# A triangular solve in 32x32 diagonal blocks in place of 64x64 chunks, and an MLP loop written out

## The chip, the cores and the metric

The kernel runs on one core of a Trainium2 chip. Its time is device microseconds (us) of one execution; the kernel before takes 2452.07 us, the median of three runs (2451.09 to 2452.88). The core has a matrix engine (TensorE, PE in the rows, with its weight loads shown apart as PEld), VectorE (DVE), ScalarE (ACT), GpSimd (POOL) and SyncE (SP), which issues the DMAs.

## What is computed

Two transformer-like layers run over 256 tokens of width 2048, all in float32. The first holds a gated delta rule (8 heads of 128), a Fourier branch, and an MLP of width 8192; the second holds a spatial gate, a state space model and an attention over a memory. The part that the change touches is the delta rule, and there the solve:

```
def gated_delta_rule_chunked(q, k, v, g, beta):      # chunks of 64 tokens
    ...
    m = jnp.where(strict, jnp.einsum("bhnid,bhnjd->bhnij", kb, k) * decay, 0.0)
    a_mat = m + jnp.eye(CHUNK, dtype=m.dtype)
    rhs = jnp.concatenate([v * beta, kb * jnp.exp(gc)[..., None]], axis=-1)
    sol = lax.linalg.triangular_solve(a_mat, rhs, left_side=True, lower=True, unit_diagonal=True)
```

There are 4 chunks of 64 tokens, 8 heads and two directions (the reverse one runs over flipped tokens): 64 triangular matrices of 64x64, each with ones on its diagonal. The kernel inverts each and multiplies by the inverse in the scan. The MLP is `x + square(relu(h @ w_mlp_up)) @ w_mlp_down`.

## The kernel before

All weights stream from HBM once, in 396 units of 512 rows by 512 columns (1 MB). SyncE loads a unit into one of four buffers `raw`; ScalarE rounds it into `w_hi` (line 820), VectorE makes the rest `w_lo` (line 1272), and TensorE multiplies each unit in 24 matmuls of 128x512 (lines 2098 to 2100: high by high, low by high, high by low; two tiles of 128 tokens). All engines walk the same list of units, `n` from 0 to 395. Between the two halves of a unit each engine runs the steps that `schedule()` put at that place; `delta_steps(half)` is the list of the delta rule's steps, and it is run twice, for heads 0 to 3 and 4 to 7 (`half`). So in each engine's queue the solve is a short group of instructions between matmuls of the weight stream.

The inverse X of a unit lower triangular matrix is built by doubling. With the blocks of size s already inverted, X of size 2s is X - X M' X, where M' is what M has in the lower left s x s block of each 2s block. `LEVELS` is (1, 2, 4, 8, 16, 32). Level 0 is done with a mask (`turn`, lines 1584 to 1599 on VectorE: unit minus masked M, for X and for its transpose). Each of the levels n = 1 to 5 has two steps:

- `solve_y` (TensorE line 2291): Y = M'X, for t = 0 and 1. GpSimd has masked M' with `level` beforehand (line 1190), ScalarE copies Y out of PSUM (line 1019).
- `solve_x` (line 2300): two products for each t, XMX transposed and XMX, and VectorE subtracts both (lines 1606 and 1609), since both X and its transpose are needed on the next level. On the last level the transposed one alone is made, and GpSimd scales it into `solT` (line 1195), which the scan reads.

One t holds two chunks, one in partitions 0 to 63 and one in 64 to 127, and 8 columns of blocks (4 heads, 2 directions). `by_chunk` (line 2256) issues for each of the 8 the two chunks' products, 16 matmuls of 64x64 for one t. The chunk in the lower partitions uses one quarter of TensorE's array and the other the quarter diagonally across. A float32 matmul of this kind is recorded as two passes, each a weight load and a matmul: 16 matmuls are x32 in the rows. `turn` on TensorE transposes M and the matrix ATT with `by_chunk` against the identity, before level 1.

Every group begins by waiting for semaphores (`take_bank` for one of the four PSUM banks, then the operands). Once they are met TensorE's queue runs it with nothing between.

The MLP is cut in 8 pieces. Of its units, 96 are run as a loop in hardware (`drive`, `LOOP0`, `LOOPS` = 3 turns of `LOOP_UNITS` = 32 units); waits in it add the turn's number times a constant to their value, and a few waits are left out in it.

Of the kernel before, what the change touches and what calls it, by code (L numbers as in the profile page):

```python
# [40 lines left out]
LEVELS = (1, 2, 4, 8, 16, 32)  # L41
MAGIC = 12582912.0
# [52 lines left out]
def end(name, n):  # L95
# [15 lines left out]
         ("chunk", 256), ("upto", 192), ("unit", 64), ("level", 896),  # L111
# [10 lines left out]
def mask_constants():  # L122
# [10 lines left out]
    out["unit"] = packed(r == c)  # L133
    out["level"] = np.concatenate([packed(x) for m in lower for x in (m.T, m)] +
                                  [packed(lower[0]), packed(lower[0].T)], 1)
# [29 lines left out]
def schedule():  # L165
# [67 lines left out]
    put(end("w_mlp_up", 2 * p), "hidden", p, 0)  # L233
    put(end("w_mlp_up", 2 * p + 1), "hidden", p, 1)
# [48 lines left out]
LOOP0 = FIRST[INDEX[("w_mlp_up", 2)]]  # L283
LOOP_UNITS = 32
LOOPS = 3


class Side:
# [3 lines left out]
    def __init__(self, key, eng, sems, old, new):  # L292
        self.key, self.eng, self.sems, self.old, self.new = key, eng, sems, old, new
        self.count, self.it, self.per = 0, None, None
# [8 lines left out]
    def _in_loop(self, key, value):  # L303
        return value if self.it is None else value + self.it * self.per[key]

# [3 lines left out]
    def at(self, *names):  # L309

        marks = [self.old[n] if self.old else ("act", 1) for n in names]
        assert len({key for key, _ in marks}) == 1, names
        return self._in_loop(marks[0][0], max(value for _, value in marks))

    def here(self):

        assert self.count > 0
        return self._in_loop(self.key, self.count)
# [5 lines left out]
def build(nc, t_in, out, old, new):  # L324

    with ExitStack() as ctx:
# [25 lines left out]
        small = take("small", [P, NSMALL - 896])  # L352
        levels = take("levels", [P, 896], mybir.dt.bfloat16)
# [13 lines left out]
        level = levels[:, :].rearrange("p (n d c) -> p n d c", d=2, c=64)  # L367
# [31 lines left out]
        level_in = at("level_in", bb + 16 * KB, [P, 896])  # L399
# [105 lines left out]
        by_head = lambda mask: mask.unsqueeze(2).broadcast_to([P, 2, 4, 64])  # L505
# [72 lines left out]
        def value(me, static, per):  # L578
            return static if me.it is None else static + me.it * per

        def drive(me, slot_work, after_loop):

            n = 0
            while n < UNITS:
                if n == LOOP0:
                    start = me.count
                    me.per = {k: v for k, v in (old or {}).get("per", {}).items()} if old else \
                        {"act": 0, "dve": 0, "pe": 0, "pool": 0}
                    with me.eng.Fori(0, LOOPS) as it:
                        me.it = it  # L590
                        for m in range(LOOP_UNITS):
                            slot_work(n + m)
                    me.it = None
                    per = me.count - start
                    new.setdefault("per", {})[me.key] = per
                    me.count += per * (LOOPS - 1)
                    for j in range(2):
                        for key, x in (("act", "hi"), ("dve", "lo")):
                            if me.key == key:
                                new[f"hidden{NPIECE - 2}.{j}.{x}"] = (key, me.count)  # L600
                                for k in range(NT):
                                    new[f"hidden{NPIECE - 2}.{j}.{k}.{x}"] = (key, me.count)
                    after_loop()
                    n += LOOPS * LOOP_UNITS
                    continue
                slot_work(n)
                n += 1

        def run_steps(me, steps, place):
            if 2 * LOOP0 <= place < 2 * (LOOP0 + LOOP_UNITS):  # L610
                local = (place - 2 * LOOP0 - 1) / 2
                for s, piece, j in ((4, 1, 0), (8, 1, 1), (20, 2, 0), (24, 2, 1)):
                    if local == s:
                        steps["hidden"](piece, j)
                return
# [12 lines left out]
        def _(sp):  # L628
            me = Side("sp", sp, done, old, new)

            def weight(n, it=None):

                if n >= RAW:
                    value = n - RAW + 1
                    sp.wait_ge(pe_used, value if it is None else value + it * LOOP_UNITS)
                if it is None:
                    src = t_in["w"][n]
                else:
                    src = t_in["w"][bass.ds(n + it * LOOP_UNITS, 1)].rearrange("a p n -> (a p) n")
                sp.dma_start(raw[:, n % RAW, :], src).then_inc(landed[n % RAW], 16)  # L640
# [141 lines left out]
            n = 0  # L782
            while n < UNITS:
                if n == LOOP0:
                    with sp.Fori(0, LOOPS) as it:
                        for m in range(LOOP_UNITS):
                            weight(n + m + RAW, it)
                    n += LOOPS * LOOP_UNITS
                    run_steps(me, steps, 2 * n)
                    run_steps(me, steps, 2 * n + 1)  # L790
                    continue
# [6 lines left out]
                n += 1  # L798
                if n != LOOP0 and n not in ends:
                    run_steps(me, steps, 2 * n)  # L800
                    run_steps(me, steps, 2 * n + 1)
# [8 lines left out]
        def _(act):  # L810
# [4 lines left out]
            def split(n):  # L815

                act.wait_ge(landed[n % RAW], value(me, 16 * (n // RAW + (n % RAW > 0)), 16 * LOOP_UNITS // RAW))
                if n >= HIGH:
                    act.wait_ge(pe_used, value(me, n - HIGH + 1, LOOP_UNITS))
                act.activation(w_hi[:, n % HIGH, :], raw[:, n % RAW, :], ACT.Copy)\  # L820
                   .then_inc(hi_split, 1)
# [7 lines left out]
            def job(tag, j):  # L829
# [9 lines left out]
                if mode == "square":  # L839
                    if ts_user[k] and me.it is None:  # L840
# [37 lines left out]
            def empty(i):  # L878
# [3 lines left out]
                act.wait_ge(pe_used, value(me, FIRST[i + 1], LOOP_UNITS))  # L882
                norm = "x" if i <= INDEX[("w_gate_a", 3)] else "mlp" if name == "w_mlp_up" else \
                    "mem" if name.startswith("xa_w") else "pre"
                if n == 0 and me.it is None:
# [118 lines left out]
            def turn(half):  # L1004
# [4 lines left out]
                for t in range(NT):  # L1009
                    act.wait_ge(pe_done, me.at(f"turn{half}{t}.Q"))  # L1010
# [3 lines left out]
            def solve_y(half, n):  # L1014
                for t in range(NT):
# [3 lines left out]
                    act.activation(per_chunk(t)[MAT], bank_of(f"solveY{half}{t}{n}", 0), ACT.Copy)\  # L1019
# [102 lines left out]
            def after_loop():  # L1122
                ts_user[:] = [f"hidden{NPIECE - 2}.1.0"] * 2

            drive(me, slot_work, after_loop)
# [5 lines left out]
        def _(pool):  # L1131
# [47 lines left out]
            def turn(half):  # L1179
                for t in range(NT):  # L1180
                    pool.wait_ge(act_done, me.at(f"turn{half}{t}.MT"))
                    pool.wait_ge(pe_done, me.at(f"decay{half}{t}.D"))
                    pool.tensor_tensor(pairs(per_chunk(t)[SUM]), pairs(per_chunk(t)[MATT]), by_head(level[:, 1]), ALU.mult)\
                        .then_inc(pool_done, me.done(f"solve{half}{t}1.Mt"))

            def solve_x(half, n):
                for t in range(NT):
                    if n < len(LEVELS) - 1:
                        pool.wait_ge(pe_done, me.at(f"solve{half}{t}{n}.Y"))
                        pool.tensor_tensor(pairs(per_chunk(t)[SUM]), pairs(per_chunk(t)[MATT]), by_head(level[:, n + 1]),  # L1190
                                           ALU.mult).then_inc(pool_done, me.done(f"solve{half}{t}{n + 1}.Mt"))
                    else:
                        pool.wait_ge(dve_done, me.at(f"solve{half}{t}{n}.XT", f"bk1{half}"))
                        for d in range(2):
                            pool.tensor_tensor(solT[:, t, 4 * d:4 * d + 4], pairs(per_chunk(t)[EXP])[:, d],
                                               wide(bk1[:, nt(t, d)], 64), ALU.mult)\
# [60 lines left out]
            for n in range(UNITS):  # L1257
                if not LOOP0 <= n < LOOP0 + LOOP_UNITS:
                    run_steps(me, steps, 2 * n)
                    run_steps(me, steps, 2 * n + 1)  # L1260
# [3 lines left out]
        def _(dve):  # L1264
# [4 lines left out]
            def split(n):  # L1269

                dve.wait_ge(hi_split, value(me, n + 1 - EARLY, LOOP_UNITS))
# [141 lines left out]
            def empty(i):  # L1413
# [3 lines left out]
                dve.wait_ge(pe_used, value(me, FIRST[i + 1], LOOP_UNITS))  # L1417
                if me.it is not None or name[:10] == "w_mlp_down" or name == "w_o":

                    dve.wait_ge(dve_emptied, value(me, emptied(i, "dve") - NT, 8 * NT))  # L1420
# [163 lines left out]
            def turn(half):  # L1584
                dve.wait_ge(dve_done, me.here())
                for t in range(NT):
                    w = per_chunk(t)
                    dve.tensor_tensor(pairs(w[INV]), pairs(w[MAT]), by_head(level[:, 6]), ALU.mult)\
                        .then_inc(dve_done, me.done())
                    dve.wait_ge(act_done, me.at(f"turn{half}{t}.MT"))  # L1590
                    dve.tensor_tensor(pairs(w[EXP]), pairs(w[MATT]), by_head(level[:, 0]), ALU.mult)\
                        .then_inc(dve_done, me.done())
                dve.wait_ge(dve_done, me.here())
                for t in range(NT):
                    w = per_chunk(t)
                    dve.tensor_tensor(eight(w[INV]), many(cols["unit"], 8), eight(w[INV]), ALU.subtract)\
                        .then_inc(dve_done, me.done(f"turn{half}{t}.X"))
# [979 lines left out]
```

## Time and profile before

| | us |
|---|---|
| median of 3 runs | 2452.07 |
| the profiled execution, its time | 2454.28 |
| its span, from first to last instruction | 2452.5 |
| TensorE busy | 2429.2 |
| VectorE, ScalarE, GpSimd busy | 1534.6, 1030.0, 274.8 |

The durations in the section of rows are of the one profiled execution. Its time is 1.8 us over its span and 2.2 us over the median. "Busy" for TensorE counts a matmul from its start to its end, and matmuls overlap in the pipeline, so durations of single matmuls (0.22 to 0.4 us) say nothing of the rate. The rate is read from the chain, where each piece runs from its start to the next one's.

### The profile page before, as it was taken

Reading aid. Unit: us, or ns where it says so; the run is one execution under the profiler, and the core shown is the slowest. Engines: PE = TensorE matmul, PEld = TensorE weight load, DVE = VectorE, ACT = ScalarE, POOL = GpSimd, SP = SyncE. Lnnn points to the kernel's source line nnn. Section 1 sums busy time; section 2 is a strip of 40 time slices with the busy share of each in tenths; the row PEclk is TensorE's granted clock in tenths of the full one; section 3 lists DMA queues with packets and bytes.
Section 4 is the critical chain, followed back from the end, with each engine's and each line's share of the span. In section 5 each row is a group of like instructions: output and inputs, shape, how many; then the busy total and the mean of one; then the engine's idle time right before and its main releaser. Section 6 shows DMA issues by size and latency. Waiting matters only on the chain.

```text
span 2452.5 us, 31953 instructions
## 1 busy us (share of the span) xinstructions
PE 2429.2 (99%) x13482; PEld 1996.0 (81%) x13482; DVE 1534.6 (63%) x1530; ACT 1030.0 (42%) x860; POOL 274.8 (11%) x226
## 2 busy tenths in 40 slices
PE   8999999999999999999999999999999999999998
PEld 7888888878888888888888888887777778888886
DVE  6465556557676455445445567789999955446564
ACT  4553345334344443443443434443433444544332
POOL 1002201210000000000000000054556400000000
PEclk9999999999999999999999999999999999999999
DMA  6343354346755455555555555665555576566753
GB/s 257 135 164 115 136 184 168 108 149 245 262 193 184 177 189 190 188 189 191 186 191 194 187 196 205 224 242 192 189 187 194 187 284 234 173 240 227 257 197 137
DMA packets 84220, 475.10 MB, mean 194 GB/s; under 512 B 8704, under 2 KB 8832, under 8 KB 32512
## 3 DMA queue, kind: packets, MB, share of 16 engines
q1 hardware_dynamic: 84096, 473.32, 54.2%
q8 instruction: 94, 1.54, 0.2%
q14 instruction: 30, 0.25, 0.0%
HBM read 450.21 MB, written 23.07 MB: 193 GB/s over the span
## 4 chain that ended last, share of the span: by engine, by line
PE 96%; DMA 1%; DVE 1%; ACT 1%; issue 0%; SPq 0%; DVEq 0%; ACTq 0%
PE acc L2098 29%; PE acc L2100 29%; PE acc L2099 29%; PE banks L2262 3%; PE banks L2111 2%; PE banks L2318 1%; DMA raw<-in_w 1%; PE banks L2385 1%; PE banks L2398 1%; DVE w_lo L1272 0%; ACT w_hi L820 0%; DMA av<-spilled 0%; DVE stats L1324 0%; PE banks L2438 0%; PE banks L2420 0%; PE banks L2236 0%
## 5 line engine op out<-in xcount | busy, mean ns | idle before, releaser
L1272 DVE TENSOR_TENSOR w_lo<-raw,w_hi 128x2048 fp32r<-128x2048 f32 x394 | 908.1, 2308 | 552.7 <-ACT w_hi L820 551.5
L820 ACT ACTIVATE w_hi<-raw 128x2048 fp32r<-128x2048 f32 x394 | 751.8, 1914 | 591.0 <-DMA raw<-in_w 588.8
L2098 PE MATMUL acc<-w_hi,a_hi 128*128 128x512 f32 x2112 | 840.5, 398 | 5.8 <-DVE a_lo L1308 3.1
L2099 PE MATMUL acc<-w_lo,a_hi 128*128 128x512 f32 x2112 | 824.7, 390 | 0.0
L2100 PE MATMUL acc<-w_hi,a_lo 128*128 128x512 f32 x2112 | 824.4, 390 | 0.0
L2098 PEld LDWEIGHTS acc<-w_hi,a_hi 128*128 128x128 f32 x2112 | 397.3, 188 | 104.2 <-issue 15.3
L2100 PEld LDWEIGHTS acc<-w_hi,a_lo 128*128 128x128 f32 x2112 | 397.4, 188 | 84.9
L2099 PEld LDWEIGHTS acc<-w_lo,a_hi 128*128 128x128 f32 x2112 | 397.8, 188 | 78.5
L2098 PE MATMUL acc<-w_hi,b_hi 128*128 128x512 f32 x928 | 364.2, 392 | 0.0
L2100 PE MATMUL acc<-w_hi,b_lo 128*128 128x512 f32 x928 | 361.5, 390 | 0.0
L2099 PE MATMUL acc<-w_lo,b_hi 128*128 128x512 f32 x928 | 361.2, 389 | 0.0
L2100 PEld LDWEIGHTS acc<-w_hi,b_lo 128*128 128x128 f32 x928 | 174.2, 188 | 36.5
L2099 PEld LDWEIGHTS acc<-w_lo,b_hi 128*128 128x128 f32 x928 | 174.4, 188 | 35.3
L2098 PEld LDWEIGHTS acc<-w_hi,b_hi 128*128 128x128 f32 x928 | 174.3, 188 | 35.1
L1252 POOL MEMSET c_out<- 128x2048 f32 x1 | 1.8, 1810 | 1029.1 <-DMA spilled<-stage_b 1029.1
L907 ACT ACTIVATE stage<-acc,stats 128x512 f32<-128x512 f32 x72 | 45.6, 685 | 128.3 <-PE acc L2100 123.8
L1436 DVE TENSOR_TENSOR x_rows<-x_rows,acc 128x512 f32<-128x512 f32 x72 | 46.2, 683 | 39.0 <-PE acc L2100 39.0
L1222 POOL TENSOR_TENSOR rot<-pow_a,pow_b 128x256 f32<-128x256 f32 x32 | 47.5, 1486 | 175.9 <-DVE s_out L1871 130.6
L1857 DVE TENSOR_TENSOR_SCAN prod<-rad,prod 128x256 f32<-128x256 f32 x64 | 56.9, 948 | 0.6
L2098 PE MATMUL acc<-w_hi,m_hi 128*128 128x512 f32 x128 | 50.6, 395 | 0.0
L2099 PE MATMUL acc<-w_lo,m_hi 128*128 128x512 f32 x128 | 50.5, 395 | 0.0
L2100 PE MATMUL acc<-w_hi,m_lo 128*128 128x512 f32 x128 | 50.5, 394 | 0.0
(356 smaller groups left out, 1642.4 us busy)
## 6 DMA issues: line engine op xcount, KB each, us to landing
raw<-in_w SPq DMA_DIRECT2D x395, 1024.0 KB, 4.8
spilled<-stage SPq DMA_DIRECT2D x72, 256.0 KB, 6.0
gate_in<-spilled SPq DMA_DIRECT2D x20, 512.0 KB, 5.8
x_rows<-in_x SPq DMA_DIRECT2D x4, 512.0 KB, 8.2
x_rows<-in_x SPq DMA_DIRECT2D x1, 2048.0 KB, 9.2
mem_rows<-in_mem SPq DMA_DIRECT2D x2, 1024.0 KB, 5.8
spilled<-stage_b SPq DMA_DIRECT2D x8, 256.0 KB, 5.9
out<-y_rows SPq DMA_DIRECT2D x3, 512.0 KB, 2.7
```

The lines of the kernel that those rows point to most:

```text
L820: act.activation(w_hi[:, n % HIGH, :], raw[:, n % RAW, :], ACT.Copy)\
L907: act.activation(dst, src, func, scale=rms(norm, t)).then_inc(act_emptied, 1)
L1222: pool.tensor_tensor(c_[:, g], pa[0][:, g], pb[0][:, g], ALU.mult).then_inc(pool_done, me.done())
L1272: dve.tensor_tensor(w_lo[:, n % RAW, :], raw[:, n % RAW, :], w_hi[:, n % HIGH, :].bitcast(F32), ALU.subtract).then_inc(lo_split, 1)
L1436: ins = dve.tensor_tensor(x_rows[:, t, cs], x_rows[:, t, cs], src, ALU.add)
L1857: dve.tensor_tensor_scan(pr[z + 1][:, g], r_, pr[z][:, g], 0.0, ALU.mult, ALU.add)\
L2098: pe.matmul(o, hi[:, tk], wh, start=first, stop=False)
L2099: pe.matmul(o, hi[:, tk], wl, start=False, stop=False)
L2100: ins = pe.matmul(o, lo[:, tk], wh, start=False, stop=last)
L2111: ins = pe.transpose(b[:, q * P:(q + 1) * P], src(q), ident)
L2262: ins = pe.matmul(b[rs, cs], lhs[rs, cs], rhs(k, rs), start=True, stop=True)
L2318: ins = pe.matmul(b(d, rs)[:, hd * P:(hd + 1) * P], lhs(d, t, rs, hd), rhs(d, rs, hd), start=True, stop=True)
```

## The change

The matrices are cut in their 32x32 diagonal blocks up to level 4, and TensorE takes each block as a matmul of its own. A 128-partition tile holds four strips of 32 partitions, so four blocks lie on the array's diagonal. Levels 1 to 4 need no more than the diagonal blocks, and `by_block` makes 32 matmuls of 32x32 where `by_chunk` made 16 of 64x64. The last level has one block product for each matrix and goes by `across`, which reads one strip and writes its neighbour: 16 matmuls of 32x32. `turn` now makes the transposed blocks, copies of the blocks, and (`turnC`) the lower left blocks transposed.

VectorE has X and its transpose side by side in one tile of 512 columns, and subtracts both in one instruction for each t (two before). ScalarE copies 256 columns of Y instead of 512, GpSimd masks 256 instead of 512. GpSimd clears `solT` on level 1 and scales the diagonal blocks into it in 8 instructions on 32 partitions after level 4; VectorE scales the last level's blocks into it in 8 more. The mask constants shrink from 896 to 384 columns. `drive` now writes all units out, with all waits.

```diff
-        level = levels[:, :].rearrange("p (n d c) -> p n d c", d=2, c=64)
+        level0 = levels[:, 0:128].rearrange("p (x c) -> p x c", c=32)
+        level = lambda n: levels[:, 64 + 64 * n:128 + 64 * n].rearrange("p (d c) -> p d c", c=32)
+        strip = lambda g: slice(32 * g, 32 * g + 32)
...
-        def drive(me, slot_work, after_loop):
...
-                    with me.eng.Fori(0, LOOPS) as it:
...
+        def drive(slot_work):
+            for n in range(UNITS):
                 slot_work(n)
...
+            def by_block(b, at, lhs, rhs):
+                for k in range(8):
+                    for g in range(4):
+                        ins = pe.matmul(b[strip(g), at + 32 * k:at + 32 * k + 32], lhs(k, strip(g)), rhs(k, strip(g)),
+                                        start=True, stop=True)
+                return ins
+            def across(b, at, lhs, rhs, to):
+                for hd in range(4):
+                    for c in range(2):
+                        for d in range(2):
+                            first, second = strip(2 * c + d), strip(2 * c + 1 - d)
+                            src, dst = (first, second) if to == "second" else (second, first)
+                            ins = pe.matmul(b[dst, at + 32 * hd:at + 32 * hd + 32], lhs(d, hd, src), rhs(d, hd, src),
+                                            start=True, stop=True)
+                return ins
...
             def solve_y(half, n):
...
-                    by_chunk(b, w[SUM], lambda k, rs: w[INV][rs, 64 * k:64 * k + 64], f"solve{half}{t}{n}.Y")
+                    if n < LAST:
+                        ins = by_block(b, 0, lambda k, rs: block_of(w[SUM], k, rs), lambda k, rs: x_n(w, k, rs))
+                    else:
+                        ins = across(b, 0, lambda d, hd, rs: block_of(w[MAT], hd, rs), lambda d, hd, rs: x_n(w, 4 * d + hd, rs),
+                                     "second")
...
             def solve_x(half, n):
...
+                    if n < LAST:
+                        by_block(b, 0, y, lambda k, rs: x_t(w, k, rs))
+                        ins = by_block(b, 256, lambda k, rs: x_t(w, k, rs), y)
+                    else:
+                        ins = across(b, 0, lambda d, hd, rs: y(8 + hd, rs), lambda d, hd, rs: x_t(w, 4 * d + hd, rs), "first")
```

TensorE's queue at the first `turn`, before; `banks` is PSUM, `work_b` and `work_c` hold the matrices, `small` the identity:

```order
734 L2262 MATMUL banks<-small,work_b 64x64 x16
735 L2262 MATMUL banks<-small,work_c 64x64 x16
736 L2262 MATMUL banks<-small,work_b 64x64 x16
737 L2262 MATMUL banks<-small,work_c 64x64 x16
738 L2098 MATMUL acc<-w_hi,a_hi 128x512
```

and the same place of the changed kernel:

```order
734 L2245 MATMUL banks<-small,work_b 32x32 x32
735 L2245 MATMUL banks<-work_b,small 32x32 x32
736 L2245 MATMUL banks<-small,work_c 32x32 x32
737 L2245 MATMUL banks<-work_c,small 32x32 x32
738 L2256 MATMUL banks<-small,work_b 32x32 x16
739 L2256 MATMUL banks<-small,work_c 32x32 x16
740 L2219 MATMUL banks<-small,work_b 64x64 x16
741 L2219 MATMUL banks<-small,work_c 64x64 x16
742 L2055 MATMUL acc<-w_hi,a_hi 128x512
```

The two groups that transpose M (32 matmuls of 64x64) have become 160 of 32x32; those of ATT stay, behind them.

TensorE's queue at level 1, `solve_y` and then `solve_x` with the weight stream between, before:

```order
750 L2262 MATMUL banks<-work_b 64x64 x16
751 L2262 MATMUL banks<-work_c,work_b 64x64 x16
752 L2098 MATMUL acc<-w_hi,a_hi 128x512
...
763 L2100 MATMUL acc<-w_hi,a_lo 128x512
764 L2262 MATMUL banks<-work_b 64x64 x32
765 L2262 MATMUL banks<-work_b,work_c 64x64 x16
766 L2262 MATMUL banks<-work_c,work_b 64x64 x16
```

and of the changed kernel:

```order
754 L2245 MATMUL banks<-work_b 32x32 x64
755 L2055 MATMUL acc<-w_hi,a_hi 128x512
...
766 L2057 MATMUL acc<-w_hi,a_lo 128x512
767 L2245 MATMUL banks<-work_b 32x32 x64
768 L2245 MATMUL banks<-work_b,work_c 32x32 x32
769 L2245 MATMUL banks<-work_c,work_b 32x32 x32
```

The places and the 12 matmuls between them are the same; 32 matmuls have become 64, and 64 have become 128.

## Rows read from the trace of the kernel before

**Rows 1.** The page: engines, busy us and share; granted clock; the code's own DMA queue.

```profile
PE 2429.2 (99%) x13482; PEld 1996.0 (81%) x13482; DVE 1534.6 (63%) x1530; ACT 1030.0 (42%) x860; POOL 274.8 (11%) x226
...
PEclk9999999999999999999999999999999999999999
...
q8 instruction: 94, 1.54, 0.2%
```

**Rows 2.** Waits of TensorE: who waited for whom, us, times, longest.

```profile
PE banks L2111 <- DMA small<-in_small: 4.8, 1, 4.8
PE acc L2098 <- DVE a_lo L1308: 3.1, 1, 3.1
PE acc L2098 <- DVE w_lo L1272: 2.4, 2, 1.9
PE banks L2111 <- ACT hidden L907: 1.4, 1, 1.4
```

**Rows 3.** The chain of waits, 170 to 260 us: start, us, what; the first half's solve.

```profile
172.35 0.87 PE banks L2245 x8
...
191.32 3.88 PE banks L2262 x128
...
195.20 0.43 PE acc L2098
...
198.15 2.01 PE banks L2262 x64
...
203.11 3.88 PE banks L2262 x128
...
250.73 2.01 PE banks L2262 x64
...
255.69 2.01 PE banks L2262 x64
```

**Rows 4.** Line 2262 alone in four stretches: length, PE busy, PEld busy, clock, DMA.

```profile
sum 140.00, PE 62.75 PEld 59.87; mean PE 15.69 PEld 14.97
```

**Rows 5.** Line 2262: its idle time before it, over the whole run.

```profile
  issue: 8.1, 23
  DVE work_b L1596: 0.4, 1
```

**Rows 6.** Timelines of ScalarE, VectorE and GpSimd at solve steps: start, us, engine.

```profile
200.21 0.60 ACT L1019 ACTIVATE work_c<-banks 128x512 f32<-128x512 f32 x1 [0.34 <-PE banks L2262]
...
257.44 1.28 DVE L1606 TENSOR_TENSOR work_b<-work_b,banks 128x512 f32<-128x512 f32 x2
...
258.20 4.38 POOL L1195 TENSOR_TENSOR solT<-work_b,nrm 128x256 f32<-128x256 f32 x4 [18.51 <-DVE work_b L1606]
```

**Rows 7.** The chain at the scan's first step, 264 to 268 us.

```profile
266.09 1.02 PE banks L2318 x16
```

**Rows 8.** Timeline, ScalarE at 43 us and TensorE at 48 us.

```profile
43.17 0.94 ACT L916 ACTIVATE levels<-level_in 128x896 bf16<-128x896 f32 x1
...
48.30 0.50 PE L2098 MATMUL acc<-w_hi,a_hi 128*128 128x512 f32 x1 [0.49 <-DVE w_lo L1272]
```

**Rows 9.** All engines around the loop's three turns, columns as in rows 4.

```profile
957.00:982.00 25.00, 25.00 (x112) 20.71 (x111) 13.07 (x9) 9.59 (x5) 0.00 (x0) 1.00 0.51 184
1135.00:1160.00 25.00, 25.00 (x112) 20.72 (x111) 13.27 (x9) 9.46 (x5) 0.00 (x0) 1.00 0.52 189
1312.00:1338.00 26.00, 26.00 (x116) 21.56 (x115) 13.55 (x9) 9.59 (x5) 0.00 (x0) 1.00 0.53 190
```

**Rows 10.** All engines in stretches near a clock drop, and in a solve step.

```profile
96.40:99.98 3.58, 3.58 (x30) 3.43 (x30) 0.05 (x1) 0.07 (x1) 0.00 (x0) 1.00 0.42 117
99.98:103.39 3.41, 3.41 (x18) 3.41 (x18) 0.42 (x1) 1.07 (x4) 0.00 (x0) 0.50 0.46 190
203.10:206.50 3.40, 3.40 (x119) 3.40 (x120) 3.10 (x3) 0.00 (x0) 0.00 (x0) 1.00 0.67 226
```

**Rows 11.** TensorE's timeline before that drop.

```profile
97.12 0.95 PE L2191 MATMUL banks<-sc,small 128*128 128x8 f32 x8
```

More of the change, by code:

```diff
@@ L41 @@
 LEVELS = (1, 2, 4, 8, 16, 32)
+LAST = len(LEVELS) - 1
 MAGIC = 12582912.0
@@ L132, in mask_constants @@
     out["upto"] = np.concatenate([packed(r <= c), packed(r >= c), packed(r <= c)], 1)
-    out["unit"] = packed(r == c)
-    out["level"] = np.concatenate([packed(x) for m in lower for x in (m.T, m)] +
-                                  [packed(lower[0]), packed(lower[0].T)], 1)
+    quarter = lambda m: np.concatenate([m[0:32, 0:32]] * 4, 0)
+    first = lower[0]
+    out["unit"] = quarter(r == c)
+    out["level"] = np.concatenate([quarter(x) for x in (first.T, first, first, first.T)] +
+                                  [quarter(x) for m in lower[1:5] for x in (m.T, m)], 1)
     out = {k: v.astype(np.float32) for k, v in out.items()}
@@ L232, in schedule @@
     put(end(f"w_mlp_down{p}", 2) - 2, "load_g_final")
-    put(end("w_mlp_up", 2 * p), "hidden", p, 0)
-    put(end("w_mlp_up", 2 * p + 1), "hidden", p, 1)
+    for p in range(1, NPIECE):
+        put(end("w_mlp_up", 2 * p), "hidden", p, 0)
+        put(end("w_mlp_up", 2 * p + 1), "hidden", p, 1)
     put(end("xa_wv", 1) + 2, "ssm_small", 0)
@@ L351, in build @@
             b_lo.append(take(f"b{i}_lo", [P, KW, T], F32R))
-        small = take("small", [P, NSMALL - 896])
-        levels = take("levels", [P, 896], mybir.dt.bfloat16)
+        small = take("small", [P, NSMALL - 384])
+        levels = take("levels", [P, 384], mybir.dt.bfloat16)
         ts = take("ts", [P, 2, NW])
@@ L781, in _ @@
             ends = {FIRST[i + 1] - 1: i for i in SPILLS}
[L782 to L791, printed above, removed]
+            for n in range(UNITS):
                 if n + RAW < UNITS:
@@ L797, in _ @@
                     run_steps(me, steps, 2 * n + 1)
[L798 to L801, printed above, removed]
+                if n + 1 not in ends:
+                    run_steps(me, steps, 2 * n + 2)
+                    run_steps(me, steps, 2 * n + 3)
             for t, n0, n1 in FINAL_DVE:
@@ L1009, in turn @@
                 for t in range(NT):
+                    act.wait_ge(pe_done, me.at(f"turn{half}.C"))
+                    act.activation(per_chunk(t)[MAT][:, 0:P], bank_of(f"turnC{half}", 0)[:, t * P:(t + 1) * P], ACT.Copy)\
+                        .then_inc(act_done, me.done(f"turn{half}.Cc"))
+                for t in range(NT):
                     act.wait_ge(pe_done, me.at(f"turn{half}{t}.Q"))
```

209 lines of the change are left out of this document (91 added, 118 removed).

## Prediction, made before the changed kernel was run

> **What bounds the kernel now.** I read the engines' busy times first: TensorE is busy for 2429.2 of 2452.5 us, the next engine for 1534.6 [rows 1]. The list of waits says the same from the other side: other engines make TensorE wait some 12 us in all, and its four longest waits are not at the solve [rows 2]. So a microsecond taken from TensorE's queue is a microsecond of the end, and one taken from another engine is worth nothing unless TensorE waits for it. The question is then what the solve's pieces cost in TensorE's queue. That stands in the chain of waits, where each piece lasts until the next begins [rows 3]. A group of x64 takes 2.01 us and one of x128 takes 3.88. The difference is 64 more passes in 1.87 us, 29.2 ns a pass, and 0.14 us is left for the start of a group. For each half there are one x128 for `turn`, five x64 for `solve_y`, four x128 and a last x64 for `solve_x`; both halves together are 2 x (5 x 3.88 + 6 x 2.01) = 62.9 us, and the sum of line 2262 over these stretches is 62.75 [rows 4]. Before a group stands a gap called "issue", some 0.35 us each (8.1 us in 23) [rows 5]. It comes with each change to these shapes and back.
>
> **What a pass of 32x32 costs.** No row has one. Two do bound it. In the 64x64 groups two tiles of the array work at once, so each tile takes 58.4 ns for a pass of 64 columns. A transpose of 128 columns on one whole tile takes 0.87 us / 8 = 109 ns [rows 3]. So 64 columns more cost 50 ns, and 32 columns fewer than 64 should give 33 ns by that line; with the two clocks per column at 2.4 GHz that it suggests, 58.4 - 26.7 = 32 ns. Four tiles share that: 8 ns a pass. That is the lower end, if the array sets the rate. The upper end is the 29.2 ns of the 64x64 pass itself, if what it pays for is handing a weight load and a matmul to the array, which a smaller tile doesn't shorten. The point where nothing is won: the change puts 1984 passes of 32x32 in each half (turn 320, levels 1 to 4 4 x 384, last level 128) for 960 of 64x64, so 960 x 29.2 / 1984 = 14.1 ns, less 0.1 for the added group start.
>
> I take 8 ns. The 58.4 ns of the 64x64 pass are explained by its columns with 5 ns to spare, as the 109 ns are by theirs with 2, so I see no room in them for an issue cost that decides. But this only shows that issuing is not slower than 29.2 ns a pass; it is not seen faster anywhere, since no shape in the trace asks for it. Both ends stay in the range.
>
> The Trainium skill has a sentence for each end. "TensorE: Matmul & The Clock Gate", Part 3, has matmuls on different tiles start about 4 ns apart, which is under 8 and would leave the array's figure. Its Part 2, "Back-to-back issue gap", puts a floor of about 25 ns on start to start for up to 64 columns, however small they are; if that floor holds over all tiles and not in each, the change gains nothing and costs 2 x (1984 x 25 - 960 x 29.2) ns, an estimate of +43 us. The trace's 29.2 ns is over that floor and so settles nothing.
>
> **The change part by part,** at 8 ns:
>
> - `solve_y`, levels 1 to 4, 8 groups: 128 passes x 8 + 0.14 = 1.16 us instead of 2.01: -0.85 each, -6.8.
> - `solve_x`, levels 1 to 4, 8 groups: 256 x 8 + 0.14 = 2.19 instead of 3.88: -1.69 each, -13.5.
> - Last level, 4 groups: 64 passes each, 0.65 instead of 2.01: -1.36 each, -5.4.
> - `turn`, 2 groups: 320 x 8 + 0.14 = 2.70, then the 64 passes that stay at 29.2 = 1.87, with one more change of shape between, 0.3 (from the 0.35 of [rows 5]): 4.87 instead of 3.88, +2.0 together.
> - Sum on TensorE: -23.7 us. At 29.2 ns a pass the same terms are +1.87 x 8, +3.74 x 8, 0 and +7.7 x 2: +60.3 us.
>
> *What hides the rest.* VectorE subtracts once for each t where it did twice (0.69 each); ScalarE copies half of Y; GpSimd masks half. None is won: TensorE has 12 matmuls of the weight stream, 2.7 us, between two groups, and the copy begun at 200.21 is done at 200.81, while `solve_x` starts at 203.11 [rows 3, 6]. When the groups get shorter, this distance does not: copy and subtraction start with each t's group and end less than 1 us behind the last, against the 2.7 us. So nothing becomes late there. Cost 0; if that cover were gone, a wait would be at most one copy of 0.6 us in each of 20 groups.
>
> *The way into the scan.* Before, GpSimd scales `solT` from 258.20 to 262.58 and TensorE first reads it at 266.09 [rows 6, 7]. Now GpSimd has its 8 instructions of 128x256 at a quarter of the partitions (at 0.6 to 1.1 us each by that row, up to 8.8 us with their clearing ahead), but they can start a level earlier, some 11 us before. VectorE has 8 small ones behind the last group; 1.28 us for two of 512 columns bounds them near 0.2 to 0.7 each, 1.6 to 5.6 us. At the upper end TensorE would wait for them from about 264 to 265 us, still before its first read. VectorE's next `w_lo` moves by as much, and TensorE works one to two units behind it, 5.4 us each. Cost 0, bound 0 to +2.
>
> *The start.* ScalarE rounds the masks in 0.94 us for 896 columns, and the chain runs through it to a stall of TensorE of 0.49 us at 48.30 [rows 8]. With 384 columns about 0.5 us goes from it: -0.4, between 0 and -0.9 with the smaller load ahead of the weights.
>
> *The loop written out.* In the stretches of 25 us across each of the loop's turns TensorE is busy for all of them [rows 9]; its queue hides what the jump costs. So nothing is won. The waits that come back are on transposes and units long done. What is added is code to load: some 4100 instructions for the tiles and two more turns of the loop's, against 94 packets in 1.54 MB before at 0.2% of the DMA engines [rows 1]. A third more of that is 0.1%. Cost 0; bound 0 to +2, if a load comes late in the tight groups, where code is used up to four times faster.
>
> *The sum:* 2454.3 - 23.7 - 0.4 = 2430.2 us for the profiled execution. That one stands 2.2 us over the median, so 2428 us for the median: 1% faster.
>
> **The rivals.**
>
> 1. *Issue decides (slower).* TensorE cannot be handed a weight load and a matmul every 8 ns, and a pass of 32x32 costs what one of 64x64 does, or near it. For it: the best rate in the whole trace is 29.2 ns for the two, in all 24 groups alike, and the change doubles their number. Against it: the columns explain those 29.2. By its upper price +60.3 us, 2512 us for the median; it decides from 14 ns a pass on. Its sign in the trace would be that groups of 32x32 cost the same for each pass whatever the number of tiles.
> 2. *Issue takes a part.* Between 8 and 14 ns, at 11 say: 3968 x 3 ns = 11.9 us of the gain are gone, 2440 us.
> 3. *Near 14 ns,* or waits that eat all of it: 2452 us. That the changes are hidden anyhow is ruled out by TensorE's 99%.
> 4. *The clock.* The granted clock fell from 2.4 to 1.2 GHz for 3.41 us behind a stretch where TensorE was busy for all of 3.58 us, but with matmuls of 8 and 16 columns for 2.6 of them; in the 64x64 groups it did not fall [rows 10, 11]. Smaller tiles use less of the array, so it could fall behind the five long groups of each half. 3.41 us at half the clock lose 1.7 us: +17 us, 2445 us. Against it: these groups are now 2 to 3 us long and the weight stream stands on both sides.
>
> **How the numbers follow.** Chances: forecast 0.50, rival 1 0.28, rival 2 0.12, rival 3 0.06, rival 4 0.04. A difference under 0.2% (4.9 us) cannot be told from none in this kernel. Faster takes the forecast, rivals 2 and 4: 0.66. The same has rival 3: 0.06. Slower has rival 1: 0.28. The forecast's own range is 2421 to 2435: a pass between 7 and 9.5 ns, the start and the bounds at nothing above. The range for all cases must reach into rival 1 until 0.2 is left out: that one spreads from 14 ns to 29 ns, 2457 to 2512 us, and I place a third of it below 2482. So 2421 to 2482.
>
> **What would show it.** In the chain, groups of x128, x256 and x64 passes of 32x32 at 1.16, 2.19 and 0.65 us show the forecast; at 3.9, 7.6 and 2.0 they show rival 1. `turn` should read 2.7 us, a gap, and 1.9. The list of waits should have no new row of TensorE at the scan or the solve. The stall at 48 us should be shorter or gone. In the stretches of the MLP TensorE should be as busy as before. Granted clock under 1.00 between 190 and 260 us would speak for rival 4. I would be wrong in the cause, even with the right time, if the groups cost as before and the gain stood elsewhere.

## The result, and the profile of the changed kernel

The changed kernel takes 2487.12 us (median, 2485.98 to 2490.56) beside 2452.48 for the kernel before: ratio 1.0143, 95% interval 1.0129 to 1.0157. It is slower by 1.4%, where 1% faster was forecast. Its profiled execution took 2485.98 us, with a span of 2484.2 against 2452.5.

The page, with the rows that answer to [rows 1]:

```profile
PE 2424.1 (98%) x15530; PEld 1988.3 (80%) x15530; DVE 1518.8 (61%) x1518; ACT 1025.3 (41%) x864; POOL 263.2 (11%) x232
...
PEclk9998999899999999999999999999999999999999
...
q8 instruction: 123, 2.02, 0.3%
```

TensorE is busy for 5 us less in a span that is 32 us longer. So it stands still, and in two slices of the span its granted clock is lower. Its list of waits (us in total, times, longest) has a first row that [rows 2] don't have:

```profile
PE banks L2245 <- issue: 34.4, 13, 5.2
PE banks L2068 <- DMA small<-in_small: 4.9, 1, 4.9
PE acc L2055 <- DVE a_lo L1273: 3.5, 1, 3.5
PE acc L2055 <- DVE w_lo L1237: 2.2, 1, 2.2
PE banks L2219 <- DVE work_b L1554: 1.5, 1, 1.5
```

Line 2245 is the matmul in `by_block`. The releaser is "issue": no semaphore and no engine ended these waits. The chain of waits shows them among groups that are nearly as short as forecast (start us, us, what):

```profile
190.00 1.30 PE banks L2245 x90
191.30 5.16 issue
196.46 0.92 PE banks L2245 x39
...
206.40 1.28 PE banks L2245 x100
...
210.67 1.57 PE banks L2245 x116
212.24 2.21 issue
...
218.41 1.28 PE banks L2245 x98
...
227.73 2.97 issue
```

TensorE's timeline shows that a wait stands inside a group, not ahead of it:

```profile
206.33 1.35 PE L2245 MATMUL banks<-work_b 32*32 32x32 f32 x128
...
210.60 1.29 PE L2245 MATMUL banks<-work_b 32*32 32x32 f32 x128
211.74 0.50 PE L2245 MATMUL banks<-work_b,work_c 32*32 32x32 f32 x37
214.45 0.41 PE L2245 MATMUL banks<-work_b,work_c 32*32 32x32 f32 x26 [2.21 <-issue]
```

The first row is `solve_y` of level 1, 128 passes, 1.28 us in the chain. The second is `solve_x` for t = 0, 128 passes, and 1.14 us behind its start that of t = 1 begins (third row). It stops after 37 passes for 2.21 us, and goes on. Nothing in the program stands at that place. But counted from TensorE's first instruction, all seven pauses of the first half end at an instruction number of 256k + 194 or 195. Queue q8 carries TensorE's code in packets of 16,384 bytes, which is 256 instructions, a *page* of code from here on.

After the pauses the granted clock falls. Three of the stretches, all engines (stretch, length, busy us of PE, PEld, DVE, ACT and POOL, clock, DMA share, GB/s):

```profile
193.10:203.30 10.20, 5.36 (x192) 5.21 (x191) 2.33 (x3) 1.64 (x4) 2.07 (x2) 0.50 0.07 27
...
244.20:251.00 6.80, 5.22 (x38) 4.19 (x39) 2.89 (x2) 0.00 (x0) 0.00 (x0) 0.50 0.01 2
264.70:271.50 6.80, 6.28 (x77) 4.78 (x77) 0.69 (x1) 0.00 (x0) 2.43 (x4) 0.50 0.01 2
```

Behind them the passes and the weight stream's matmuls stand further apart, until the clock is back. In all, 51.2 us of the solve and what follows it are at 1.2 GHz in the changed kernel; in the kernel before the only such stretches of its body were 3.41 us at 100 and at 2008 us.

I summed the time from each matmul's start to the next, by kind, from 150 to 2480 us of each trace (a pause counts whole, with the pass ahead of it). The second row is passes on 64x64 tiles, with the scan's 256 of 128 columns, some 16 us in each column. These are the terms, in us, for the two kernels and two of the experiments below:

| | before | after | e3 | e6 |
|---|---|---|---|---|
| 32x32 passes | 0 | 39.2 | 40.1 | 25.9 |
| passes on 64x64 tiles | 83.3 | 27.6 | 24.4 | 27.2 |
| pauses in or behind these | 0 | 39.8 | 22.4 | 0.7 |
| all else | 2207.8 | 2216.0 | 2216.5 | 2210.7 |
| sum, against before | | +31.5 | +12.3 | -26.6 |
| span, against before | | +31.7 | +12.4 | -26.3 |

The tiles do bring 16.5 us (83.3 - 39.2 - 27.6). The pauses take 39.8, 1.5 of it a wait for VectorE at `turn`. "All else" grows by 8.2, in which 63 more matmuls of the weight stream at half the clock (439 ns each, not 230) are 13 and the others give some 5 back.

### The profile page after: what moved, and what is told of

The parts are those of the page before. It is cut to its first block, busy times and chain, and to the rows that moved or that the text cites. A ratio compares the mean times of both kernels' runs of the same rounds, so it can differ in the third digit from the quotient of the medians.

```text
span 2484.2 us, 35541 instructions
## 1 busy us (share of the span) xinstructions
PE 2424.1 (98%) x15530; PEld 1988.3 (80%) x15530; DVE 1518.8 (61%) x1518; ACT 1025.3 (41%) x864; POOL 263.2 (11%) x232
## 4 chain that ended last, share of the span: by engine, by line
PE 96%; issue 2%; DMA 1%; DVE 1%; ACT 0%; SPq 0%; DVEq 0%; ACTq 0%
PE acc L2055 30%; PE acc L2056 29%; PE acc L2057 29%; PE banks L2068 2%; PE banks L2245 2%; PE banks L2314 1%; PE banks L2382 1%; PE banks L2395 1%; PE banks L2219 0%; DMA av<-spilled 0%; PE banks L2435 0%; PE banks L2417 0%; PE banks L2193 0%; DMA raw<-in_w 0%; DMA spilled<-stage 0%
```

## The experiments

The theory (1): a page of code reaches TensorE some 3.5 us after TensorE has entered the page before it, and later when data is in flight. A page of 32x32 passes is used up in some 1.3 us. So TensorE stops wherever such pages follow each other. Its rivals: the written-out loop (A), the clock alone (B), a price per instruction in TensorE's own issue (C), and code that is late only because of the weights' transfers (D).

**e1, e2: the change in two halves.** e1 is the kernel before with `drive` as `for n in range(UNITS)` and no hardware loop; e2 is the kernel after with the loop kept.

```
e1:  -                    with me.eng.Fori(0, LOOPS) as it:
     +            for n in range(UNITS):
e2:  the edits to turn, solve_y, solve_x and the masks alone
```

> The kernel before, with only the MLP loop written out; the solve keeps its 64x64 tiles. Theory 1 (code supply: TensorE stands still in the groups of 32x32 because their instructions are used up faster than the next ones are loaded): the weight stream uses its code slowly, so nothing changes, 2452 us within 0.2%, and TensorE's packets of code rise by about as much as between the two kernels without a wait appearing. Rival A (the written-out loop is what costs): 2460 to 2485 us, with TensorE idle or at half clock somewhere between 950 and 1340 us.

> The kernel after, with the MLP loop kept as a loop; only the solve is changed. Theory 1: as the kernel after, 2487 us within 0.3%, with some 34 us of waits called issue on line by_block's matmuls and some 50 us at half clock. Rival A (the written-out loop, because it moves or lengthens the code): the waits are gone and the time is near 2430 us.

e1: 2451.85 us, ratio 0.9998 (0.9988 to 1.0008), no new wait, 107 packets of code for 94. e2: 2487.69 us, ratio 1.014 (1.0123 to 1.0157). Rival A is out: the loop is worth under 0.2% either way, the solve is all of it. The waits of e1 and of e2, one row each, and e1 in one of the stretches of [rows 9]:

```profile
PE banks L2047 <- DMA small<-in_small: 4.9, 1, 4.9
```

```profile
PE banks L2309 <- issue: 35.6, 13, 4.9
```

```profile
957.00:982.00 25.00, 25.00 (x112) 20.71 (x111) 13.88 (x9) 8.58 (x5) 0.00 (x0) 1.00 0.57 202
```

**e3: the same instructions, spread.**

```
-        s += [("solve_y", half, n), ("solve_x", half, n)]
+        s += [("solve_y", half, n)]
+        s += [("solve_x", half, n, ts) for ts in (((0,), (1,)) if n < LAST else ((0, 1),))]
     (and "turn" at three places: M of t = 0, M of t = 1, the rest)
```

> The kernel after, with the same instructions for the solve in smaller pieces: solve_x for t = 0 and t = 1 at two places of the schedule, turn at three (M of t = 0, M of t = 1, the rest), so that no piece has more than 256 instructions of TensorE and 12 matmuls of the weight stream stand between two. Theory 1: the code of the next piece is loaded beside the weight stream, the waits called issue fall from 34 us to under 10, half-clock stretches in the solve from 48 us to under 15, time 2435 to 2450 us, faster than before. Rival B (the clock falls because small tiles use little of the array, and the waits only go with it): the same tiles do the same work, so half-clock stretches stay near 50 us and the time above 2470. Rival C (the chip takes the instructions of 32x32 passes slower than the array does, on average 14 ns each wherever they stand): 2487 us, plus some 4 us for the added changes of shape.

2463.75 us (2458.80 to 2466.72), ratio 1.0037 (1.0023 to 1.0052). The direction is theory 1's: the same tiles and passes, 23 us less, and 20.5 us at half clock in the solve for 51.2, so B and C fall, which had nothing change. The size isn't. It was to be faster than before and is slower, and 20.6 us of pauses are left:

```profile
PE banks L2251 <- issue: 14.7, 12, 1.9
...
PE acc L2061 <- issue: 3.9, 2, 3.4
...
PE banks L2262 <- issue: 1.6, 1, 1.6
```

A piece of a page and the 12 matmuls of the weight stream behind it take 4.27 us (206.40 to 210.67 in the chain of the kernel after). Why that isn't enough, m3 shows.

**e4: half the instructions, the same columns.**

```
-                for k in range(8):
-                        ins = pe.matmul(b[strip(g), at + 32 * k:at + 32 * k + 32], ...
+                for k in range(0, 8, 2):
+                        ins = pe.matmul(b[strip(g), at + 32 * k:at + 32 * k + 64], ...
```

> The kernel after, with half the instructions in turn, solve_y and solve_x up to level 4: each 32x32 tile of weights meets 64 columns instead of 32, so that the columns that pass through the array stay the same; every second block of the solve is not computed as it should be. Theory 1: half the code for almost the same columns; groups of x64 at 0.8 to 1.3 us where x128 took 1.28; waits called issue from 34 us to under 8, time 2430 to 2445 us. Rival B (clock by the use of the array): as much use as in the kernel after, half clock stays near 50 us and the time above 2470. Rival C (an average price per instruction): half of some 80 us in the solve's groups goes, also near 2445, but with waits of half their sum, some 17 us, left.

2432.71 us, ratio 0.9919 (0.9902 to 0.9935). It leaves half of the blocks' products out, so it measures time and is no version of the kernel. Waits called issue are 8.8 us in five, and the clock's stretches nearly gone (11 matmuls of the weight stream at half clock, 71 in the kernel after). The first row was expected under 8 us in all:

```profile
PE banks L2219 <- issue: 5.5, 2, 4.2
...
PE banks L2247 <- issue: 1.9, 2, 1.0
PE banks L2258 <- issue: 1.4, 1, 1.4
```

A pass of 64 columns on these tiles cost 14.4 ns and one of 32 had cost 9.4, with the starts of the groups in both. The passes thus became cheaper by only 8 us (39.2 to 31.3); the pauses, by 30. It is the number of instructions that made them.

**e5: everything moved by half a page.**

```
+                    for k in range(8 if half == 0 else 0):      # decay's group, once more
...
+                            pe.matmul(b[rs, 64 * k:64 * k + 64], ...
```

> The kernel after, with the group of decay of the first half computed twice (64 more 64x64 passes, 128 more instructions, 1.9 us), so that everything behind stands half a page of code later. Theory 1: every wait called issue that falls in the solve stands 128 instructions earlier in the program than in the kernel after, hence in the middle of other groups, and at one and the same place within a page again; their sum is again 25 to 45 us. Rival (the waits belong to certain groups, to their semaphores or to PSUM): they stay at the matmuls where they are now.

One run, 2497.19 us beside 2454.33: 10 us more than the kernel after, of which the added group is 1.9; the waits (below) and the stretches at half clock (61.4 us for 51.2) are longer too. All seven pauses of the first half end at instruction 256k + 194 or 195 again, so in the program they stand half a page elsewhere. In the kernel after `solve_x` of level 1 stopped after 37 passes of t = 1 (above); here it stops after 101 (62, four between, 35), 64 passes or 128 instructions on:

```profile
211.57 0.71 PE L2249 MATMUL banks<-work_b,work_c 32*32 32x32 f32 x62
...
212.14 0.48 PE L2249 MATMUL banks<-work_c,work_b 32*32 32x32 f32 x35
217.40 0.63 PE L2249 MATMUL banks<-work_c,work_b 32*32 32x32 f32 x27 [4.78 <-issue]
```

The sum is 41.5 us (35.4 on `by_block`, 6.1 on `across`). In the second half too, and in e2, e3 and e4, each gap over 0.75 us between the solve's passes, or from one of them to the matmul behind it, ends at 256k + 194 or 195. That shows the pauses belong to page ends and to no group.

**m1 to m4: the resource by itself.** Small kernels with nothing but such groups. m1 has 4096 passes of 32x32 (8192 instructions) written out; m2 the same in a loop; m3 is m1 with 44 transfers of 1 MB beside it; m4 has 1024 passes of 64x64 written out. None computes anything of the reference. Each ran once.

```
m1:             for _ in range(64): group()                    # 32 matmuls of 32x32
m2:             with pe.Fori(0, 8) as it:
                    for _ in range(8): group()
m3:  as m1, and on SP  for n in range(44): sp.dma_start(raw[:, n % 4, :], ...)
m4:  as m1, with 8 matmuls of 64x64 in a group
```

> A small kernel of its own: 64 groups of 32 matmuls of 32x32 (64 passes, 128 instructions each, 8192 in all) written out one after the other, nothing beside them. Theory 1 (code supply): a page of 256 instructions takes 3.3 to 3.8 us to arrive, and only then does TensorE go on; 32 pages, 105 to 122 us for the groups, TensorE standing still for about 2.3 us in each page, and loads of code some 3.5 us apart. Rival D (the code is late only because the weight stream's transfers stand ahead of it): 1.3 us for each page, 42 us in all. Rival C (an average price per instruction in TensorE's own issue): no pauses, evenly 14 ns for each instruction or 5 ns for each.

> The same 8192 instructions, but as a loop of 8 turns over 8 groups (1024 instructions written out). Theory 1: code is loaded in the first turn alone (4 or 5 pages, 14 to 18 us), then the turns run at 9 to 10 ns a pass, 5.2 us each and their jump; 50 to 65 us in all. Rival C (TensorE's own issue): the same time as written out, whatever that is.

> The written-out kernel again, with 44 transfers of 1 MB from device memory running beside it, at most four in flight, as the weight stream has them. Theory 1 with queueing (a load of code also waits behind packets of data): the pages arrive 4 to 6.5 us apart instead of some 3.5, 130 to 200 us for the 32. If data in flight does not matter to the loads of code: the time of the kernel without the transfers, within 3 us.

> The small kernel written out with tiles of 64x64: 64 groups of 8 matmuls (16 passes, 32 instructions each, 2048 in all, 8 pages), nothing beside them. Theory 1: a page of such passes keeps TensorE busy for 128 x 29.2 ns = 3.7 us, which is what the load of the next one needs (3.7 us), so it runs with almost no pauses (under 3 us in all, 30 us for the groups), at full or half clock for the array. If the loads need 3.7 us behind the end of a page, not beside it: 3.7 us of pause in each page, 55 us.

m1's timeline of TensorE, four of its pages:

```profile
8.84 1.27 PE L60 MATMUL banks<-y_in,x_in 32*32 32x32 f32 x128 [1.43 <-issue]
...
23.48 1.93 PE L60 MATMUL banks<-y_in,x_in 32*32 32x32 f32 x128 [1.80 <-issue]
27.20 1.93 PE L60 MATMUL banks<-y_in,x_in 32*32 32x32 f32 x128 [1.80 <-issue]
30.66 1.93 PE L60 MATMUL banks<-y_in,x_in 32*32 32x32 f32 x128 [1.52 <-issue]
```

128 passes, a pause, 128 passes, all the way: 3.69 us for each page with no data in flight, 131.93 us for the kernel. The distance is as expected. The pauses are 1.4 to 2.2 us long and not 2.3, because m1 runs at half clock from 11 us on, where 128 passes last 1.93 us and not 1.27. D falls as the only cause. m2's:

```profile
4.31 3.21 PE L60 MATMUL banks<-y_in,x_in 32*32 32x32 f32 x223 [4.31 <-DMA y_in<-in_w]
8.71 1.93 PE L60 MATMUL banks<-y_in,x_in 32*32 32x32 f32 x128 [1.20 <-issue]
12.44 1.93 PE L60 MATMUL banks<-y_in,x_in 32*32 32x32 f32 x128 [1.80 <-issue]
16.45 33.73 PE L60 MATMUL banks<-y_in,x_in 32*32 32x32 f32 x3523 [2.08 <-issue]
```

The first turn is m1. After it 3523 passes run on with nothing between them but some 0.3 us at each turn's jump, 62.7 us for the kernel. From 22 us on they stand 9.0 ns apart, the jumps included. From 16.5 to 21.9 us they stand 13 ns apart, as in m1, and there too no page end stops them (401 passes, three pages): the clock doesn't make the pauses. The same instructions, twice as fast: rival C is out for good. The packets of code, of m1 and of m2:

```profile
q8 instruction: 32, 0.52, 1.8%
```

```profile
q8 instruction: 4, 0.07, 0.5%
```

m3's pages, and the last ones when its transfers have ended:

```profile
35.80 1.93 PE L60 MATMUL banks<-y_in,x_in 32*32 32x32 f32 x128 [4.00 <-issue]
41.99 1.93 PE L60 MATMUL banks<-y_in,x_in 32*32 32x32 f32 x128 [4.26 <-issue]
...
150.72 1.93 PE L60 MATMUL banks<-y_in,x_in 32*32 32x32 f32 x128 [1.80 <-issue]
154.45 1.93 PE L60 MATMUL banks<-y_in,x_in 32*32 32x32 f32 x128 [1.80 <-issue]
```

6.1 us a page beside data, 3.7 without, 177.90 us for the kernel, as theory 1 with queueing expected. The records of the packets say which part grows. In m1 a packet begins mostly 1.1 us after TensorE has gone on, and TensorE can enter that page 2.3 to 2.9 us later; in m3 it begins 3.4 to 3.8 us after, and the rest is the same 2.3 to 2.6. So the load's start is late behind data, its length isn't. The kernel after has both cases: at 189.97 us it enters a page while weights flow, the packet begins at 194.07 and TensorE goes on at 196.46, 6.5 us; from 197.50 on, with its buffers full and no weights in flight, the packets begin 0.8 to 1.2 us after and the next page comes 3.3 us behind. A page that lasts longer lets a second packet come: the one entered at 218.54 lasts 6.8 us, packets begin at 219.42 and 223.18, and the page entered at 225.32 then runs through in 1.1 us without a pause. That corrects e3's expectation: a page had little over 4 us and needed up to 6.1.

m4 ran without one pause:

```profile
4.16 32.52 PE L60 MATMUL banks<-y_in,x_in 64*64 64x64 f32 x1024 [4.16 <-DMA y_in<-in_w]
```

```profile
10.00:36.00 26.00, 26.00 (x899) 26.00 (x896) 0.00 (x0) 0.00 (x0) 1.00 0.02 4
```

It took 48.71 us. Up to 9.6 us a pass takes 53 ns, as 64x64 passes do at half clock in the kernel after; behind that 29.2 ns, 3.73 us a page, with no pause at seven page ends. Loads overlap use, and 64x64 passes use a page no faster than it comes. So the 64x64 tiles of the kernel before stood right at this limit, and that hid it from its trace.

**e6 to e8: a version that beats both.** X is kept transposed only, and VectorE turns its 32x32 blocks. TensorE loses half of `solve_x` and the diagonal part of `turn`, so its code for each half is 2432 instructions, not 3968.

```
-                        by_block(b, 0, y, lambda k, rs: x_t(w, k, rs))
-                        ins = by_block(b, 256, lambda k, rs: x_t(w, k, rs), y)
+                        ins = by_block(b, 0, y, lambda k, rs: x_t(w, k, rs))
 (VectorE)
+                        dve.tensor_tensor(w[EXP][:, 0:256], w[EXP][:, 0:256], b[:, 0:256], ALU.subtract)
+                        dve.transpose(w[EXP][:, 256:512], w[EXP][:, 0:256])
e6:  an empty place behind each group of a level, none ahead of turn
e7:  the places of the kernel after
e8:  e6, one of the empty places put ahead of turn again
```

> A version meant to beat both: the solve by 32x32 blocks as in the kernel after, but X is kept as X transposed alone, and VectorE turns the 32x32 blocks (its transpose, 128x256 in one instruction) into X; so solve_x has half its matmuls, and the diagonal blocks of turn need none. TensorE's code for each half falls from 3968 to 2432 instructions (9.5 pages), and a second place of the weight stream stands behind each group of a level, so that a page has some 6.5 us. Theory 1: a page needs 3.7 us alone and 6.2 beside the stream, so at most 10 us of waits called issue are left; passes in 32x32 cost 23 us, in 64x64 27, instead of 83 us for all in the kernel before; 2420 to 2432 us. Rival E (VectorE's chain of subtraction and transpose comes late for the next group): a wait of TensorE for VectorE on work tiles in the list of waits, over 10 us in all, and no gain.

> The same with the schedule of the kernel after, so one place of the weight stream (2.7 us) between most groups of the solve: a page of code has some 4.5 us. Theory 1: between 3.7 and 6.2 us for a page, so waits called issue come back in part, 8 to 20 us, with some half clock, 2425 to 2440 us; slower than the version with two places by 3 to 12 us.

> The version with VectorE's transposes and two places, but with the empty place ahead of turn put back (it comes from behind solve_y of level 1): VectorE then has one place more for decay before TensorE wants its blocks. Expected: the 6.3 us that TensorE waited for VectorE at turn go, all or but for 1 us, and some 1 to 2 us of waits called issue may come at level 1; 2421 to 2426 us.

| | median us | ratio to before | waits: issue | for VectorE at the solve |
|---|---|---|---|---|
| e6 | 2428.34 | 0.990 (0.9883 to 0.9916) | 0.8 | 6.3 |
| e7 | 2428.77 | 0.9901 (0.9885 to 0.9918) | 5.9 | 3.4 |
| e8 | 2428.62 | 0.9906 (0.9889 to 0.9922) | 0.8 | 7.4 |

All three are 1% faster than the kernel before and 2.4% faster than the one after. e6 was as forecast, but rival E took part: the pauses are gone, and VectorE makes TensorE wait. e8's forecast (2421 to 2426) failed: I took one empty place from `solve_y` of level 1 to shelter `turn`, and the wait moved there. The row in e6, then in e8:

```profile
PE banks L2269 <- DVE work_c L1542: 6.3, 2, 3.1
```

```profile
PE banks L2258 <- DVE work_b L1568: 6.5, 2, 3.2
```

What comes late differs. In e6 it is VectorE's `decay`, which masks M (L1542): it ends at 184.35 and TensorE's `turn` starts at 184.40. VectorE's own `turn`, 6.6 us from 184.98 to 191.55, comes just in time there. In e8 it is this `turn` that is late, since a `w_lo` of 2.28 us went ahead of it. Rows of VectorE in e6, then in e8 (x4 and x2 are sums):

```profile
183.67 0.68 DVE L1542 TENSOR_TENSOR work_c<-banks,work_c 128x512 f32<-128x512 f32 x1
...
184.98 1.84 DVE L1553 STREAM_TRANSPOSE work_b<-work_b 32x256 f32<-32x256 f32 x4
```

```profile
187.92 1.83 DVE L1553 STREAM_TRANSPOSE work_b<-work_b 32x256 f32<-32x256 f32 x4
...
193.72 0.77 DVE L1568 STREAM_TRANSPOSE work_b<-work_b 128x256 f32<-128x256 f32 x2
```

e7, with fewer places, has 5.9 us of issue but only 3.4 us of waits for VectorE; my expectation that it be 3 to 12 us slower than e6 was wrong for that reason. Both places at once, ahead of `turn` and behind `solve_y` of level 1, weren't tried.

## Why the prediction was wrong, step by step

**What bounds the kernel.** Right: TensorE. The terms of its queue meet the change of the span within 0.3 us in the kernel after, e3 and e6 (table above).

**What a pass of 32x32 costs.** Nearly right. Inside a group at full clock the passes stand 8.6 to 9.1 ns apart, for a forecast 8, and with the groups' starts they cost 9.4 (39.2 us less 4.8 at half clock, over 3660 passes). `solve_y` takes 1.28 us for a forecast 1.16. Rivals 1 and 2 looked for the danger at this place, and it isn't there: m2 hands TensorE a weight load and a matmul every 9.0 ns. The Trainium skill ("TensorE: Matmul & The Clock Gate", Part 2, "Back-to-back issue gap") had a floor of about 25 ns from start to start, by which nothing would be won; over four tiles the trace doesn't show it, and e4's 14.4 ns for 64 columns doesn't either.

**The sum on TensorE.** At a forecast -23.7 us the passes gave -16.5. The 32x32 passes took 39.2 us where the forecast's groups sum to 34.8 (8 x 1.16 + 8 x 2.19 + 4 x 0.65 + 2 x 2.70). About half of these 4.4 us is the dearer pass, and half of them the some 300 passes at half clock. The other 2.8 us are the 64x64 passes of ATT: the first half's 64 took 3.65 us at half clock, for a forecast 1.87.

**"The loop written out."** Its first part, nothing for the loop, is right (e1: 0.9998). The step that failed is its last sentence: "Cost 0; bound 0 to +2, if a load comes late in the tight groups, where code is used up to four times faster." The term was mis-sized. It is 39.8 us of pauses and, as their consequence, some 9 to 13 us of clock. It also stood under the wrong edit, since the loop has nothing to do with it. I had seen the packets of code at 0.2% of the DMA engines [rows 1] and read that share as the cost. But the share says how much the transfers load the engines, not how long TensorE waits for one. The number that was missing is a latency: 3.7 us from one page to the next. It could have been bounded from the trace of before. There 128 passes of 64x64, a page's worth, last 128 x 29.2 ns = 3.74 us without a pause [rows 3], so its supply was known to keep up with 3.74 us once, and with nothing faster. (The pages cut where the pauses stand: one lasts 3.72 us, from 217.54 on, the next shortest 4.61 and 6.42.) The change asked for 1.28. That is the reasoning by which I held "issue decides" open for passes ("it is not seen faster anywhere"), and I didn't apply it to code.

The Trainium skill ("Runtime: NRT & Kernel Launch", "Instruction fetch mechanics") has the next 16 KiB fetched while the current one runs and calls the cost of a boundary mostly hidden. The first half is what m4 shows; the second holds for 64x64 passes (no pause in 8 pages) and not for 32x32, where each of m1's boundaries but the first costs 1.4 to 2.2 us.

**Rival 4, the clock.** It was put at 0.04 and ruled out for the reason that the weight stream stands on both sides. The clock did fall, and the reason was another one: it falls behind pauses. In e6 and e7 the same small tiles run with few pauses, and 5 and 21 matmuls of the weight stream are at half clock, for 71. Nor does it take a pause for code: in e6 the clock is at 0.50 from 183.50 to 190.00, and TensorE had stood still for VectorE for 3.13 us, until 184.40. No run has the pauses without the clock, so its share of 9 to 13 us rests on the sums in the table alone.

**What hides the rest, the scan, the start.** No wait for ScalarE, VectorE or GpSimd came at the solve but one of 1.5 us at `turn`'s groups of ATT, behind a pause and at half clock. GpSimd's eight scalings and VectorE's small ones brought no wait at the scan. At the start ScalarE's rounding takes 0.51 us, not 0.94, and TensorE's stall of 0.49 us at 48.30 [rows 8] has no counterpart from 40 to 50 us; what that brought the whole is too small to be told from the rest.

## What to carry to other kernels

When a change makes instructions shorter or more numerous on the bounding engine, divide the code's bytes by the time they last: here a page of 256 TensorE instructions must last some 3.7 us, or 6.1 beside full weight traffic, over more than one page in a row. Below that, write fewer instructions, put slow ones between them (e4 and e6 show the first, e3 and e6 the second), or keep the piece in a hardware loop (m2 alone shows it; it wasn't tried in the kernel). A pause of the bounding engine with the releaser "issue", inside a group and at equal distances in instructions, is this case; the DMA share of the code's queue doesn't show it.

## What the runs showed of the hardware beyond that

- A loop body of 1024 instructions (64 KB) stays where it is: m2 loaded 4 packets for 32 pages' worth of instructions. So there is room for at least four pages, yet in m1 a single packet comes for each page entered, 1.1 us after. Why it begins 2.6 us later beside the 1 MB transfers stays open; that it does, is m1 against m3.
- In m1 the granted clock fell to half at 11 us and stayed there, with TensorE busy for 52.47 of the 100 us from 20 to 120; in m2 it was 1.00 with 24.41 busy of the 25 us from 25 to 50. A pass of 32x32 takes 13 ns at half clock (1.93 us for 128, less the last one's 0.24) and 9 at full, so half the clock doesn't double its price.
- The granted clock in the rows reads 1.00 also where the trace has no record of it: m3 has none at all, m2 none before 22.0 us, m4 none before 9.6 us. The passes there stand 13 ns (32x32) and 53 ns (64x64) apart, as at half clock. So a short kernel's clock is better read from the distance of its passes.
- VectorE's transpose of 32x32 blocks costs 0.45 us for 128x256 in float32, about as much as a subtraction of that size (0.42). On 32 partitions four of them take 1.84 us: as long each as on 128.
